# Projection, filters and gates as one stage that walks one list of steps

## What is computed

```python
h = rmsnorm(x, norm1_g)
proj = h @ w_in
cp = dwconv3(proj[..., :CONV_CH], conv_w, conv_b)

# hyena_filter_spectrum(L, ...)
h = jnp.sin(fr1 * (z @ w1 + b1))
h = jnp.sin(fr2 * (h @ w2 + b2))
h = (h @ w3).reshape(L, 2, HY_ORDER, HY_WIDTH)
h = h * jnp.exp(-t * deltas)[:, None, None, :]
kern = jnp.concatenate([h[:, 0], zeros((1, ...)), h[:0:-1, 1]], axis=0)
kern = kern * lax.rsqrt(jnp.sum(jnp.square(kern), axis=0, keepdims=True))
return jnp.fft.rfft(kern, axis=0)

# hyena_mix
def long_conv(z, ks, d):
    zf = jnp.fft.rfft(z, n=2 * L, axis=1)
    return jnp.fft.irfft(zf * ks[None], n=2 * L, axis=1)[:, :L] + d * z
z = x1 * long_conv(v, kspec[:, 0], bias[0])
return x2 * long_conv(z, kspec[:, 1], bias[1])
```

## Time and profile before

| | us |
|---|---|
| median of 3 runs | 2763.15 |
| lowest, highest | 2758.42, 2766.29 |
| profiled execution | 2759.94 |
| its span (first to last instruction) | 2758.3 |

### The profile page before, as it was taken

One profiled execution on the slowest core, in us unless ns is written; L12 is line 12 of the kernel. 1 busy time (PEld: TensorE's weight loads), 2 busy tenths in 40 slices (PEclk: granted clock), 3 DMA queues, 4 the chain that ended last, 5 costly groups with the idle time before them and its releaser, 6 DMA issues. The chain is left out here.

```text
span 2758.3 us, 26967 instructions
## 1 busy us (share of the span) xinstructions
PE 2365.0 (86%) x10324; PEld 1903.1 (69%) x10324; DVE 1159.3 (42%) x1504; ACT 727.6 (26%) x1047; POOL 262.1 (10%) x174
## 2 busy tenths in 40 slices
PE   5999999934797578877778789999999996699898
PEld 4888888811585467656556578888888885588686
DVE  4222221155777277765623433333333333322332
ACT  5222221123222333334312332111221121312321
POOL 0000000003334043232000000000000000000000
PEclk9999999965898799989789889999999998899999
DMA  4222222213132676654244211111111111534542
GB/s 131 77 76 65 76 69 69 73 39 97 35 65 65 216 224 177 195 172 136 65 160 152 63 42 53 55 59 53 53 53 61 64 53 44 154 105 115 152 140 83
DMA packets 189030, 264.78 MB, mean 96 GB/s; under 512 B 11127, under 2 KB 133879, under 8 KB 188568
## 3 DMA queue, kind: packets, MB, share of 16 engines
q1 hardware_dynamic: 177704, 214.18, 26.6%
q0 software_dynamic: 10096, 46.40, 4.6%
q10 hardware_dynamic: 1152, 3.15, 0.3%
HBM read 171.21 MB, written 67.32 MB: 86 GB/s over the span
## 5 line engine op out<-in xcount | busy, mean ns | idle before, releaser
L128 PE MATMUL up_acc<-up_h_hi,up_w_hi 128*128 128x512 f32 x1056 | 412.0, 390 | 3.0 <-DVE up_w_lo L474 3.0
L130 PE MATMUL up_acc<-up_h_hi,up_w_lo 128*128 128x512 f32 x1056 | 411.8, 390 | 0.0
L129 PE MATMUL up_acc<-up_h_lo,up_w_hi 128*128 128x512 f32 x1056 | 411.8, 390 | 0.0
L245 DVE SCALAR_TENSOR_TENSOR up_u<-up_acc,up_conv_par,up_u 128x1023 f32<-128x1023 f32 x88 | 85.4, 1012 | 463.2 <-ACT up_u L462 463.2
L128 PE MATMUL in_acc<-in_h_hi,in_w_hi 128*128 128x512 f32 x696 | 273.0, 392 | 3.1 <-DVE in_w_lo L343 3.1
L130 PE MATMUL in_acc<-in_h_hi,in_w_lo 128*128 128x512 f32 x696 | 271.4, 390 | 0.0
L129 PE MATMUL in_acc<-in_h_lo,in_w_hi 128*128 128x512 f32 x696 | 271.4, 390 | 0.0
L128 PE MATMUL down_acc<-down_w_hi,down_s_hi 128*128 128x512 f32 x528 | 209.6, 397 | 53.7 <-DVE down_w_lo L640 41.4
L128 PEld LDWEIGHTS up_acc<-up_h_hi,up_w_hi 128*128 128x128 f32 x1056 | 198.9, 188 | 44.7 <-issue 3.4
L129 PEld LDWEIGHTS up_acc<-up_h_lo,up_w_hi 128*128 128x128 f32 x1056 | 198.9, 188 | 41.4
L130 PEld LDWEIGHTS up_acc<-up_h_hi,up_w_lo 128*128 128x128 f32 x1056 | 198.8, 188 | 41.4
(11 more groups left out here) (234 smaller groups left out, 3575.7 us busy)
## 6 DMA issues: line engine op xcount, KB each, us to landing
down_s_raw<-g_scratch SPq DMA_DIRECT2D x24, 1408.0 KB, 6.8
up_w_raw<-arg_w_up_t SPq DMA_DIRECT2D x44, 512.0 KB, 3.5
g_scratch<-up_prod POOLq DMA_DIRECT2D x22, 768.0 KB, 3.5
in_w_raw<-arg_w_in_t SPq DMA_DIRECT2D x29, 512.0 KB, 3.6
tok_scratch<-in_out POOLq DMA_DIRECT2D x16, 768.0 KB, 4.9
mix_classes<-mix_split SPq DMA_DIRECT2D x48, 256.0 KB, 4.8
mix_kf<-k_scratch SPq DMA_DIRECT2D x48, 256.0 KB, 2.9
mix_split<-mix_classes SPq DMA_DIRECT2D x48, 256.0 KB, 4.8
```

The costliest lines, as they stand in the source:

```text
L128: pe.matmul(out, w_hi, x_hi, start=first, stop=False)
L129: pe.matmul(out, w_hi, x_lo, start=False, stop=False)
L130: return pe.matmul(out, w_lo, x_hi, start=False, stop=last)
L245: dve.scalar_tensor_tensor(u[:, t0 + 1:t0 + n], acc[:, t0:t0 + n - 1], w_prev, u[:, t0 + 1:t0 + n], ALU.mult, ALU.add).then_inc(half_step, 1)
```

## The change

Input projection, hidden layer, gates and filters become one stage, `projections_filters_and_gates`. A planner writes one list `schedule`, and every engine walks it in order and does its part of each step.

- The projection runs by sequence: first the 29 column tiles with the 1024 tokens of sequence 0 (48 matmuls a tile), then again with the 512 tokens of sequence 1 (24 a tile). So the weights are loaded and split twice. Only the 8 token tiles of sequence 0 are normed ahead; the other 4 come after column tile 24. The norm of a tile is listed as scale, turn, turn, with no skew between tiles. ScalarE waits at its head for all of the first loads.
- The hidden layer's steps stand among the norm tiles: argument 0 after tile 3, sine 0 and the second matmul after tile 5, argument 1, sine 1, the move of h2 and its split after tile 7. Behind them comes the first product step.
- The filters are 8 jobs (order, sequence, half of the channels). Sum and difference are formed on the weights w3 instead of on the taps, so one VectorE operation gives both decayed taps; POOL only adds up the squares. Tap matmuls have 256 columns and share one PSUM bank with the power sum. Each job ends its taps with the power sum, root, reciprocal and bias row; then come 8 stage parts of 4 operations, and then 8 transforms. VectorE's copy out of PSUM multiplies by 1/norm, and the skip term d is added to tap 0 of the sum (divided by the scale). k goes out through a ring of 3 buffers, two transfers for each transform. The filter steps are strewn over product steps of column tiles 1 to 23, by weights.
- The gates are steps beside the products of sequence 1, from its fifth tile on.
- In the mix stage the root, reciprocal, `prepare`, and the scratches for scale and power are gone; a join is one operation.

The diff, cut to its core:

```diff
+TILE_ORDER = [MIX_V_O[:N_CONV - N_QK + N_V] + [N_KINDS - 1] + MIX_V_O[N_CONV - N_QK + N_V:] + list(range(N_QK)),
+              [N_KINDS - 1] + MIX_V_O + list(range(N_QK))]
...
+    filters = []
+    for o in range(ORDER):
+        if o == 0:
+            filters.append(("split_w3", 0.5, o))
+        for c in [c for c in range(len(jobs)) if jobs[c][0] == o]:
+            s = jobs[c][1]
+            size = sns[s] / 2
+            for tt in range(nts[s]):
+                filters.append(("tap", 0.6, c, tt))
+                if tt:
+                    filters.append(("square", 0.2, c, tt - 1))
+            filters += [("square", 0.2, c, nts[s] - 1), ("power", 1.0, c)]
+            filters += [("stage", 1.5 * size, c, ri, part) for ri in (1, 0) for part in range(4)]
+            last = c == len(jobs) // ORDER - 1
+            if last:
+                filters.append(("load_w3", 0, 1))
+            for cls in range(CLASSES):
+                filters += [("load_tab", 0, c, cls)]
+            for cls in range(CLASSES):
+                filters += [("transform", 3.6 if s == 0 else 1.0, c, ri, cls) for ri in range(2)]
+            if last:
+                filters.append(("split_w3", 0.5, 1))
...
+    def projection(i):
+        s, k = tiles[i]
+        after = []
+        if i:
+            b = i - 1
+            kind = kind_of(b)
+            after = [[("centre", 0, b)] if kind in ("qk", "mix") else [], [("gather", 0, b)], []]
+            if kind in ("mix", "v"):
+                after += [[("turn", 0.5, b, q)] for q in range(nts[tiles[b][0]] // quad)]
+            else:
+                after += [[("finish", 0, b)]]
+            after += [[("store", 0, b)]]
+        out = []
+        for kt in range(KD):
+            if i < len(tiles):
+                if kt == 0 and i + 2 < len(tiles):
+                    out.append(("load_w", 0, i + 2))
+                out.append(("product", 1.4 if s == 0 else 0.7, i, kt))
+                if kt == 2 and i + 1 < len(tiles):
+                    out.append(("split_w", 0, i + 1))
+            out += after[kt] if kt < len(after) else []
+        return out
...
+    for k in range(nts[0]):
+        put(norm_of(k))
+        if k + 3 < nts[0]:
+            put([("load_x", 0, k + 3)])
+        if k == 3:
+            put([("argument", 0, 0)])
+        if k == 5:
+            put([("sine", 0, 0), ("hidden", 0, 1)])
+    put([("argument", 0, 1), ("sine", 0, 1), ("move_h2", 0), ("split_h2", 0)])
+    upto = 24
+    window = sum(x[1] for i in range(1, upto) for x in projection(i))
+    share = sum(x[1] for x in filters) / window
+    credit, spent, at = 0.0, 0.0, 0
+    late = [("load_x", 0, nts[0]), ("load_x", 0, nts[0] + 1)]
+    for k in range(nts[0], TT):
+        late += norm_of(k) + ([("load_x", 0, k + 2)] if k + 2 < TT else [])
+    first1 = n0 + 3
+    step1 = 0
+    for i in range(len(tiles)):
+        for n, x in enumerate(projection(i)):
+            put([x])
+            if 1 <= i < upto:
+                credit += share * x[1]
+                while at < len(filters) and spent < credit:
+                    put([filters[at]])
+                    spent += filters[at][1]
+                    at += 1
+            if i == upto - 1 and n == len(projection(i)) - 1:
+                put(filters[at:])
+                at = len(filters)
+                put([("drain_k", 0)])
+            if upto <= i < n0 and late and x[0] == "product":
+                put(late[:1])
+                late = late[1:]
+            if i == n0 - 1 and n == len(projection(i)) - 1:
+                put(late)
+                late = []
+            if i == first1 and n == 0:
+                put([("load_gates", 0)])
+            if i > first1 + 1 and x[0] == "product" and x[3] % 4 == 0 and step1 < len(gates):
+                put([gates[step1]])
+                step1 += 1
+    put(gates[step1:])
...
+                def transform(c, ri, cls):
+                    v = trans_at[c, ri, cls]
+                    if v:
+                        store_k(v - 1)
+                    if ri == 1 and cls + 2 < CLASSES:
+                        load_tab(c, cls + 2)
+
+                def drain_k():
+                    store_k(len(trans_at) - 1)
+                    for b in range(outs):
+                        sp.wait_ge(k_stored[b], 32 * len(range(b, len(trans_at), outs)))
+                    sp.wait_ge(sem["added"], taps_before[-1])
+
...
+                def tap(c, tt):
+                    o, s, half = jobs[c]
+                    if tt == 0:
+                        pe.wait_ge(sem["h2_low"], 1)
+                        pe.wait_ge(sem["w3_low"], o + 1)
+                    free(("tap", c, tt))
+                    rows = slice(SEQS[s][0] + tt * P, SEQS[s][0] + (tt + 1) * P)
+                    cols = slice(half * HC, (half + 1) * HC)
+                    for x in range(2):
+                        dst = cbank[:, 0, x * HC:(x + 1) * HC]
+                        pe.matmul(dst, h2[:, rows], w3_hi[:, x, cols], start=True, stop=False)
+                        last = pe.matmul(dst, h2[0:HID, rows], w3_lo[:, x, cols], start=False, stop=True)
+                    last.then_inc(sem["tapped"], 1)
+
+                def power_sum(c):
+                    pe.wait_ge(sem["added"], taps_before[c + 1])
+                    free(("power", c))
+                    for x in range(2):
+                        last = pe.matmul(cbank[:, 0, 0:HC], ones[:, :], power[:, x, :], start=x == 0, stop=x == 1)
+                    last.then_inc(sem["summed"], 1)
+
+                def transform(c, ri, cls):
+                    o, s, half = jobs[c]
+                    s_n, v, n = sns[s], trans_at[c, ri, cls], c * CLASSES + cls
+                    pe.wait_ge(sem["staged"], 2 * (c + 1))
+                    pe.wait_ge(tab_loaded[n % 2], 16 * (n // 2 + 1))
+                    if v >= 2:
+                        pe.wait_ge(sem["k_copied"], v - 1)
+                    terms = [(0, cr[0]), (2, sn[0])] if ri == 0 else [(1, cr[1]), (0, sn[1])]
+                    for kb in range(s_n):
+                        for i, (which, src) in enumerate(terms):
+                            for sb in range(s_n):
+                                last = pe.matmul(cbank[:, 1 + v % 2, kb * HC:(kb + 1) * HC], tab[n % 2][:, which, sb, kb, :], src[:, cls, sb, :],
+                                                 start=i == 0 and sb == 0, stop=i == 1 and sb == s_n - 1)
+                    last.then_inc(sem["k_ready"], 1)
...
+                def root_of(c):
+                    n = SEQS[jobs[c][1]][1]
+                    act.wait_ge(sem["summed"], c + 1)
+                    if c:
+                        act.wait_ge(sem["biased"], 2 * c)
+                    act.activation(root[:, :], cbank[:, 0, 0:HC], ACT.Sqrt, scale=0.5 * n * n).then_inc(sem["rooted"], 1)
...
+                def decayed_tap(c, tt):
+                    m = taps_before[c] + tt
+                    dve.wait_ge(sem["tapped"], m + 1)
+                    dve.wait_ge(sem["decay_ready"], m + 1)
+                    if tt == 0 and c:
+                        dve.wait_ge(sem["staged"], 2 * c)
+                    last = dve.tensor_tensor(both[:, :, tt, :], cbank[:, 0, :].rearrange("p (x c) -> p x c", x=2),
+                                             decay[m % 2][:, :, :].broadcast_to([P, 2, HC]), ALU.mult)
+                    if tt == 0:
+                        last.then_inc(sem["fixed"], 1)
+                        dve.wait_ge(sem["fixed"], 2 * c + 1)
+                        dve.tensor_tensor(brow[:, :], both[0:1, 0, 0, :], both[0:1, 1, 0, :], ALU.add).then_inc(sem["fixed"], 1)
+                        dve.wait_ge(sem["fixed"], 2 * c + 2)
+                        dve.tensor_scalar(both[0:1, 0, 0, :], brow[:, :], 0.5, None, ALU.mult)
+                        last = dve.tensor_scalar(both[0:1, 1, 0, :], brow[:, :], 0.5, None, ALU.mult)
+                    last.then_inc(sem["decayed"], 1)
+
+                def add_bias(c):
+                    o, s, half = jobs[c]
+                    dve.wait_ge(sem["rooted"], c + 1)
+                    dve.wait_ge(sem["f_loaded"], 48)
+                    if c >= 2:
+                        dve.wait_ge(sem["k_copied"], per_job * (c - 1))
+                    dve.reciprocal(scale_row[c % 2][:, 0, :], root[:, :])
+                    dve.tensor_tensor(brow[:, :], root[0:1, :], bias[:, o, half * HC:(half + 1) * HC], ALU.mult).then_inc(sem["biased"], 1)
+                    dve.wait_ge(sem["biased"], 2 * c + 1)
+                    dve.wait_ge(sem["squared"], taps_before[c + 1])
+                    dve.scalar_tensor_tensor(both[0:1, 0, 0, :], brow[:, :], 1.0 / SEQS[s][1], both[0:1, 0, 0, :],
+                                             ALU.mult, ALU.add).then_inc(sem["biased"], 1)
+
+                def stage(c, ri, part):
+                    s_n = sns[jobs[c][1]]
+                    if part == 0:
+                        dve.wait_ge(sem["decayed"], taps_before[c + 1])
```

(64 more changed lines are left out.)

1162 lines of the change are left out of this document (557 added, 605 removed).

## The result

| | before | after |
|---|---|---|
| median, us | 2763.99 | 2846.29 |
| lowest, highest | 2758.42, 2766.29 | 2843.83, 2849.2 |
| profiled execution (span) | 2759.94 (2758.3) | 2849.2 (2847.5) |
| mix stage's first transfer | 917.0 | 1044.1 |
| mix stage to output projection | 466.5 | 427.6 |

The account below looks back on a forecast made before the run. TensorE was taken to bound the projection (500.4 of 504.9 us busy). The merged stage's terms summed to 1024 against 917.0, 107 later; less 20 in the mix stage, 2759.94 + 107 - 20 = 2847 us, 8-in-10 range 2738 to 2895.

Parts of the forecast that it names:

- TensorE's work, clock included: Merged stage: products and turns 505 us, filter, gate and second-norm work 214, lower clock after long waits 25.
- first product: Start of merged stage: late loads, unskewed norm tiles and first sine put the first product at 76 us, 18 later.
- wait behind product 0: Merged stage's start: TensorE waits 9 us because VectorE does the second sine argument before splitting weight tile 1.
- taps, power sum, w3: Filter jobs: TensorE waits for VectorE at taps sharing one bank, at the power sum and w3 splits, 52 us.
- stage parts, up to the transforms: Filter jobs: root chain and VectorE's stage parts outlast the products listed beside them; TensorE waits 92 us.
- ring of stores: Small filter jobs: transforms come close together with a ring of 3 stores, costing 6 us in all.
- second sequence: Merged stage, before sequence two: SP waits for all k stores before loading x, costing TensorE 13 us.
- mix stage and behind: Mix stage: shorter joins 11 us, no POOL preparation 7, start 2; together 20 us less, between 5 and 45.
- The page: ScalarE: skill page's 2.66 us per table switch would add 13 us; the prediction went by the trace's 1.29.
- A: Merged stage: VectorE hides under products, stage ends at 915, total 2738 us, once large-job waits fall below 5; chance 0.18.
- B: Filters: k stores hold the ring of 3, x and w3 loads queue behind SP's waits; 2885 us, chance 0.15.
- C: Whole kernel: gains and losses cancel to within 8 us; 2760 us, chance 0.05.

Follow-up runs that it names:

- w_start: Kernel of weights with another start: next tile's square listed ahead, filter-rate wait, first weight split and sine arguments moved; 2730.2 us.
- weights: Changed kernel with other planner weights for tap, last square, power sum, stage part and transform, by its trace's durations; 2752.5 us, ratio to before 0.9979.
- warm: Changed kernel with 225 idle matmuls, results overwritten, where TensorE waits in the filter jobs; 2838.6 us, ratio to before 1.0299.
- tuned: Kernel of weights with w_start's start, table loads ahead of w3, second sequence's norm and gates respaced, filters strewn over tiles 1 to 25; 2692.1 us.
- Join_one: Kernel before with a mix-stage join of one VectorE operation instead of two, added z left out of the result; 2731.4 us, ratio 0.9904.
- in_block: Changed kernel with the filter steps in one row behind column tile 23 instead of strewn over products; 2945.1 us, ratio to before 1.0684.

## Why the prediction was right, and where only its sum was

The median came out at 2846.3 for a forecast of 2847, but that is in part luck. The work term was 71 us too small, and the waits at taps and stage parts together 48 too large; what this and the smaller terms left on the merged stage, 20 us, the mix stage took back with 18.

| term | forecast | measured |
|---|---|---|
| first product | 76 | 80.6 |
| TensorE's work, clock included | 744 | 815.5 |
| wait behind product 0 | 9 | 7.2 |
| taps, power sum, w3 | 52 | 28.8 |
| stage parts, up to the transforms | 92 | 67.2 |
| ring of stores | 6 | 0 |
| second sequence | 13 | 13.8 |
| gates | 23 | 16.8 |
| last product to next stage | 9 | 10 |
| first transfer of the mix stage | 1024 | 1044.1 |
| mix stage and behind | -20 | -37.9 |

The measured waits come from the list of TensorE's rests above 0.9 us and the view of its waits; 67.2 is the sum for the filters: 36.3 + 8.1 at transforms, and turns of 6.69, 6.53, 5.47 and 4.14 us. What is left of the 138.9, 5 us, is small rests, the largest a wait of 2.3 for a weight tile's low part.

**Start.** Right in kind and near in size. ScalarE did wait for the filter parameters, to 18.9 us; the tile took 5.54 us, as summed. The first argument cost 7.7 us for 7. The first product came 23 us later than in the kernel before; run w_start shows that 13 of them were to be avoided.

**Work and clock.** This is the step that failed. The transforms and the price of a tap matmul were right: 0.31 us at full clock for my 0.32, between ends of 0.22 and 0.43, in the changed kernel's timeline of TensorE:

```profile
126.30 0.39 PE L1139 MATMUL in_cbank<-filt_w_hi,filt_h_parts 128*128 128x256 f32 x1
...
126.61 0.38 PE L1140 MATMUL in_cbank<-filt_w_lo,filt_h_parts 64*128 64x256 f32 x1
```

But I charged the clock with 25 us: one wait a job "whose recovery nothing covers", 2.5 us each. The trace has 249 us at the lower level. A product there takes 0.42 to 0.43 us (111.26 to 111.68) and 0.23 at the upper level (87.00 to 87.23):

```profile
87.00 0.39 PE L130 MATMUL in_acc<-in_h_hi,in_w_lo 128*128 128x512 f32 x1
87.23 0.39 PE L128 MATMUL in_acc<-in_h_hi,in_w_hi 128*128 128x512 f32 x1
...
111.26 0.63 PE L130 MATMUL in_acc<-in_h_hi,in_w_lo 128*128 128x512 f32 x1
111.68 0.63 PE L128 MATMUL in_acc<-in_h_hi,in_w_hi 128*128 128x512 f32 x1
```

Between the changed kernel and weights, 115 us less at that level went with 43 us less of busy TensorE; by that share the 249 us are some 93, an estimate, against the 25: 68 of the 71 us by which this term was short. The rows give the same: read in windows of 1 us, TensorE is busy for some 201 us at the lower level, and products take 0.43 for 0.23 there, so that 201 x 0.20 / 0.43 = 93 are lost; for run weights the same working has 106 and 49, a difference of 44 for the 43 measured. I had counted one long wait a job with a recovery of 5 us. But the taps' short waits come with a lower clock too: the clock falls at 98 us, within the wait of 7.2 that ends at 100.73, and is back at 1.00 only at 122, with waits of 0.7, 1.75 and 0.8 us in between, 21 us for my 5. The warning was in the profile of before: the filters there show 0.85 with 43 us of rest in 258.

**Taps and stages.** Right in kind, too large in size: 52 against 28.8, 92 against 67.2. Of the 67.2 VectorE released 59.1, part of it at turns ahead of the transforms; the other 8.1 were a table load behind SP's load of w3, which my sum did not have. The reciprocal took 1.75 us (I had 1.8), and from power sum (245.06) to last stage part (272.1) the job shown above took 27 us, as summed. (32 operations at 9.7 us for 17 are 18.3 us, not the 18.8 of my sum; it changes little.) But at the lower clock the products beside it last longer and cover more, so that the mis-sized clock term and this one may in part be one error, seen from two sides. Run warm points that way: matmuls at a higher clock, 19 us less of them, and 8 us more of waits. How much of the 25 us at the stages and of the 23 at the taps goes back to this, and how much to steps that I counted as uncovered and were not, no run tells apart.

**Rivals.** A, VectorE hides, did not come in this kernel, but its condition was the right one: run weights brings a large job's waits below 5 us, and the time to that of before. I had it at 2738 from then on; weights took 2752 and tuned 2692. Of B, the ring of stores did not show: VectorE's waits for a store of k are 1.5 us in all. Its queue on SP did once, in the 8.1 us of the table load. C fell with the 127 us of the merged stage.

**Mix stage.** 38.9 for 20, inside its range of 5 to 45. The step that was off: of 22 us saved on VectorE I let TensorE see half, and I put the clock at nothing. Join_one measured 27 us: TensorE rests 18 us less, most of the 22, and is busy 10 us less at the higher clock. A join stands between a product of TensorE and its next one, so that most of what it saves is seen.

**The page.** The Trainium skill (ScalarE: Activation LUTs, What ACT_TABLE_LOAD costs) has 2.66 us for a switch. In the changed kernel's first norm tile, ScalarE:

```profile
22.10 0.19 ACT L1187 ACTIVATION_READ_ACCUMULATOR hid_xn<-hid_x_in 128x1 f32 x1
22.31 1.28 ACT L1189 ACT_TABLE_LOAD   x1
23.60 0.29 ACT L1189 ACTIVATE in_root_x<-in_sumsq,in_eps 128x1 f32<-128x1 f32 x1
```

From the end of one operation (22.29) to the start of the next it is 1.31 us. And in the job shown above the load for the root ran at 243.69, while ScalarE still waited for the power sum, so that there it cost nothing at all. The measurement decides against the dearer sum.

## What to carry to other kernels

When engines walk one common list, set the planner's weights by the durations of the engine that is late, here VectorE, with its chains of small steps counted: wrong weights alone cost 90 us here, and no engine but TensorE was near full (VectorE was busy 45% of the time). Price a rest of TensorE twice, once as rest and once for the clock that follows, but not as independent terms: at a lower clock the work beside a late engine stretches and hides part of the wait. An operation between two dependent TensorE steps can be worth nearly its full time and the clock besides, however idle its engine is on average; here a join's was.

## What the runs showed of the hardware that I had not expected

- A tap matmul of 256 columns is followed by the next in 0.31 us at full clock (and in 0.51 at half, 108.71 to 109.22), neither half nor all of the 0.43 of 512 columns.
- The granted clock went with TensorE's rests in the filter windows over all versions: 0.67 with 219 us of rest in 482 (in_block), 0.85 with 101 in 626 (the changed kernel), 0.90 with 58 in 615 (warm), 0.92 with 50 in 529 (weights), 0.95 with 25 in 493 (tuned).
- The table load for a function can run while ScalarE waits for that function's input; it is then off the path (243.69 to 244.97, the root at 247.17).
